# Attention with both heads of a pair in one step: 64-column value matmuls on the two halves of a PSUM bank, and softmax divisors summed by GpSimd and VectorE

## The chip, the cores and the metric

One core of a Trainium2 chip runs the whole program. The metric is the device time of one execution in microseconds, median of the runs.

## The reference

Two layers of a decoder trunk over 1024 tokens, width 1024, 16 heads of 64 dimensions, all in float32. Layer 0 has three attention branches that gates add up: compressed keys ("cmp"), full causal attention (every one of the 16 selected blocks is there, so the selection is the whole causal range) and a sliding window of 512 ("near"). Layer 1 is masked attention with one key and value of 64 dimensions shared by all heads, where a mask leaves each query its 256 best keys. After each attention comes an output projection and a gated ConvFFN. What the change touches is this part, of either layer:

```
s = jnp.where(mask, einsum(q, k), NEG_INF)
p = softmax(s)
o = einsum(p, v)
```

The kernel computes exp(s - peak) without dividing, sums it over the keys, and divides the product with v by that sum at the end.

## The kernel before, in words

**Tiling.** Attention goes over 16 rounds (`ROUNDS`): a round is one pair of heads and one half (512 queries) of the tokens. In a round, a branch ("rb" counts round and branch) is worked off in units. A unit is one head and one block of 128 keys against the queries that see it: 512, 384, 256 or 128 of them (`key_blocks`). In the first half a branch has 4 blocks of 512, 384, 256 and 128 queries; in the second, "full" has 8 (five of 512) and "near" 8 (two each of 512, 384, 256 and 128). A "cmp" branch is a single unit for both heads.

**A unit.** TensorE: `scores_pe` writes the scores, transposed (keys on partitions), to one of three PSUM banks by two float32r matmuls (L866 of high and L868 of low parts) and bf16 matmuls that add the mask (L872). ScalarE: `exp_act` (L910) writes the exponentials to one of four buffers PX. TensorE: `values_pe` (L890) multiplies them, in float32, by a stationary operand V of 128 columns: 64 of values and 64 of ones. So partitions 0 to 63 of the result are the product and partition 64 is the sum of the probabilities: the divisor costs no matmul of its own. The result accumulates in bank 6 or 7, by head in turn. "cmp" has its product (L884) in bank 6 and its divisors, by a matmul with ones (L885), in bank 7.

**Around it.** The order is written out by unit: at step s TensorE does the scores of unit s+2, then what the planner (`AttentionPlan`, with a cost in microseconds for each unit) has put in ring slot s, then the values of unit s. The ring is three more PSUM banks, in which TensorE computes the untransposed scores of a coming round (`peak_pe`, L813) and VectorE takes their row maxima (`peak_dve`, L1002); a transpose (L832) and a DMA put the maxima into the low query operand. When a branch closes, `evict_act` copies divisor and product per head (L933, L934, for cmp L929, L930), the SyncE queue sends the divisors through DRAM (L1092, L1097, L1103), VectorE takes the reciprocal (`sums_dve`) and applies it (`apply_dve`, L1037, L1041), and ScalarE and VectorE split the result into high and low parts HH and HL (L942, L1047) for the output projection. In layer 1 VectorE and ScalarE also finish four mask tiles during attention, at the steps of `LATE_MASKS`; VectorE's part is L2234 to L2242.

**The output projection** (`outproj_pe`) takes 16 weight tiles k. Tiles 0 and 1 are loaded before attention, 2 and 3 after it (`attention_sp`, end); GpSimd splits the first three into high and low parts (`split`, L455 and L458), ScalarE and VectorE the others (L467, L474). Before tile 4 the SyncE queue waits for the last HL and restores the 4 MB residual XT (L1109).

The value matmul, with its ones column inside V, is:

```
V = B[a.keys[n.kind][2]]
last = nc.tensor.matmul(PS[:, 6 + n.g % 2, n.c0:n.c0 + n.w], V[:, g, n.kb, :], probs,
                        start=n.first, stop=n.last)
```

## Time and profile before

| | |
|---|---|
| median of 3 runs | 3381.35 us (3377.76 to 3383.71) |
| profiled execution | 3380.0 us, its span 3378.2 us |
| attention of layer 0 in the span | 327 to 884 us |
| attention of layer 1 in the span | 2185 to 2493 us |
| TensorE busy (matmul) | 2992.9 us, 89% |
| VectorE busy | 2085.6 us, 62% |
| ScalarE busy | 1512.3 us, 45% |
| GpSimd busy | 279.4 us, 8% |
| mean granted TensorE clock | 0.937 of full speed |

PE is TensorE's matmul, PEld its weight load, DVE VectorE, ACT ScalarE, POOL GpSimd, SPq the SyncE queue that issues DMAs. A float32 matmul leaves two records of weight load and two of matmul in the trace, a float32r or bf16 matmul one of each. A record of a matmul lasts longer than the time in which it holds up the next one; the start of the next weight load or matmul tells that time.

### The profile page before, as it was taken

Reading aid. Unit: us, or ns where it says so; the run is one execution under the profiler, and the core shown is the slowest. Engines: PE = TensorE matmul, PEld = TensorE weight load, DVE = VectorE, ACT = ScalarE, POOL = GpSimd, SP = SyncE. Lnnn points to the kernel's source line nnn. Section 1 sums busy time; section 2 is a strip of 40 time slices with the busy share of each in tenths; the row PEclk is TensorE's granted clock in tenths of the full one; section 3 lists DMA queues with packets and bytes.
Section 4 is the critical chain, followed back from the end, with each engine's and each line's share of the span. In section 5 each row is a group of like instructions: output and inputs, shape, how many; then the busy total and the mean of one; then the engine's idle time right before and its main releaser. Section 6 shows DMA issues by size and latency. Waiting matters only on the chain.

```text
span 3378.2 us, 37432 instructions
## 1 busy us (share of the span) xinstructions
PE 2992.9 (89%) x13312; PEld 2299.4 (68%) x13312; DVE 2085.6 (62%) x3708; ACT 1512.3 (45%) x2609; POOL 279.4 (8%) x221
## 2 busy tenths in 40 slices
PE   7797999999879999999968664389997999999997
PEld 5685666666667888878856553256666788887885
DVE  6544445555266766677675699664326676667656
ACT  4342554455444544444433544344434454444443
POOL 2352000000000000000003035300000000000000
PEclk9787999999989999999989787689998999999999
DMA  5143211121322333333323012332132233333332
GB/s 165 44 105 97 50 47 39 42 52 36 110 75 88 95 93 100 95 92 96 98 69 96 0 54 84 94 70 54 39 104 75 88 94 94 100 95 93 99 109 73
DMA packets 360178, 270.45 MB, mean 80 GB/s; under 512 B 63942, under 2 KB 313864, under 8 KB 359480
## 3 DMA queue, kind: packets, MB, share of 16 engines
q1 hardware_dynamic: 358839, 265.96, 27.4%
q8 instruction: 106, 1.74, 0.2%
q10 hardware_dynamic: 1152, 2.10, 0.2%
q14 instruction: 81, 0.66, 0.1%
HBM read 233.46 MB, written 29.82 MB: 78 GB/s over the span
## 4 chain that ended last, share of the span: by engine, by line
PE 77%; DVE 9%; ACT 4%; issue 3%; DMA 3%; POOL 3%; SPq 1%; POOLq 0%; ACTq 0%; DVEq 0%
PE PS L485 18%; PE PS L487 18%; PE PS L486 18%; PE PS L890 10%; PE PS L813 3%; PE PS L868 3%; PE PS L866 3%; PE PS L872 2%; SPq L1912 1%; DVE m_Z L2285 1%; DVE RT_b L590 1%; DMA WL<-ql_save 1%; POOL m_QS L1929 1%; PE PS L639 1%; PE PS L884 0%
## 5 line engine op out<-in xcount | busy, mean ns | idle before, releaser
L485 PE MATMUL PS<-HH,WH 128*128 128x512 f32 (+1 forms) x2160 | 859.1, 398 | 133.9 <-POOL WL L458 90.3
L486 PE MATMUL PS<-HL,WH 128*128 128x512 f32 (+1 forms) x2160 | 850.7, 394 | 0.0
L487 PE MATMUL PS<-HH,WL 128*128 128x512 f32 (+1 forms) x2160 | 849.6, 393 | 0.0
L485 PEld LDWEIGHTS PS<-HH,WH 128*128 128x128 f32 x2160 | 415.9, 193 | 228.2 <-issue 96.9
L486 PEld LDWEIGHTS PS<-HL,WH 128*128 128x128 f32 x2160 | 415.5, 192 | 87.1 <-issue 2.5
L487 PEld LDWEIGHTS PS<-HH,WL 128*128 128x128 f32 x2160 | 414.4, 192 | 86.6
L474 DVE TENSOR_TENSOR WL<-WR,WH 128x1024 fp32r<-128x1024 f32 x290 | 354.2, 1221 | 109.4 <-ACT WH L467 97.8
L467 ACT ACTIVATE WH<-WR 128x1024 fp32r<-128x1024 f32 x290 | 308.1, 1062 | 124.4 <-PE PS L487 89.9
L910 ACT ACTIVATE n_PX<-PS 128x512 f32<-128x512 f32 (+3 forms) x400 | 186.7, 468 | 256.7 <-PE PS L872 205.3
L1002 DVE CUSTOM_DVE_ANT_0 n_JUNK<-PS,n_MZ 128x512 bf16<-128x512 f32 (+2 forms) x320 | 148.6, 488 | 134.1 <-PE PS L813 132.6
L454 POOL TENSOR_TENSOR TOUCH<-WR 128x1 f32<-128x1 f32 x45 | 12.0, 267 | 2030.4 <-PE PS L487 1031.3
L890 PE MATMUL PS<-m_PX,m_V 128*128 128x512 f32 (+3 forms) x384 | 165.5, 514 | 9.7 <-ACT m_PX L910 9.7
L890 PE MATMUL PS<-n_PX,n_VS 128*128 128x512 f32 (+3 forms) x384 | 162.5, 505 | 10.7 <-ACT n_DR L930 10.7
L1342 DVE TENSOR_TENSOR Y_c<-PS,Y_c 128x512 f32<-128x512 f32 x160 | 107.0, 688 | 88.0 <-PE PS L487 87.6
L1342 DVE TENSOR_TENSOR Y_b<-PS,Y_b 128x512 f32<-128x512 f32 x160 | 107.0, 688 | 87.3 <-PE PS L487 86.9
L910 ACT ACTIVATE m_PX<-PS 128x512 f32<-128x512 f32 x192 | 93.1, 488 | 137.5 <-PE PS L872 137.0
L1002 DVE CUSTOM_DVE_ANT_0 m_JUNK<-PS,m_MASK 128x512 bf16<-128x512 f32 (+3 forms) x160 | 89.9, 595 | 100.0 <-PE PS L813 99.9
L485 PE MATMUL PS<-HIDH_b,WH 128*128 128x512 f32 x352 | 142.4, 405 | 6.3 <-issue 3.2
L485 PE MATMUL PS<-HIDH_c,WH 128*128 128x512 f32 x352 | 141.9, 403 | 3.9 <-issue 3.2
L890 PE MATMUL PS<-n_PX,n_VW 128*128 128x128 f32 (+3 forms) x384 | 140.4, 448 | 0.0
L487 PE MATMUL PS<-HIDH_b,WL 128*128 128x512 f32 x352 | 139.8, 397 | 0.0
L486 PE MATMUL PS<-HIDL_b,WH 128*128 128x512 f32 x352 | 139.7, 397 | 0.0
(375 smaller groups left out, 5373.3 us busy)
## 6 DMA issues: line engine op xcount, KB each, us to landing
WR<-in_ffn_w_up SPq DMA_DIRECT2D x176, 512.0 KB, 3.8
WR<-in_ffn_w_down SPq DMA_DIRECT2D x88, 512.0 KB, 3.6
WH<-qh_save SPq DMA_DIRECT2D x64, 256.0 KB
n_RB<-r_save SPq DMA_DIRECT2D x96, 128.0 KB, 3.0
WR<-in_nsa_w_out SPq DMA_DIRECT2D x16, 512.0 KB, 4.1
WL<-ql_save SPq DMA_DIRECT2D x32, 256.0 KB
WR<-in_dsa_w_in SPq DMA_DIRECT2D x16, 512.0 KB, 4.4
WR<-in_dsa_w_out SPq DMA_DIRECT2D x16, 512.0 KB, 4.2
```

Source lines behind the costliest of these rows:

```text
L467: nc.scalar.activation(WH[:, x, :], WR[:, r, :], ACT.Copy).then_inc(w_hi, 1)
L474: nc.vector.tensor_tensor(WL[:, x, :], WR[:, r, :], WH[:, x, :].bitcast(F32), ALU.subtract).then_inc(w_split, 1)
L485: nc.tensor.matmul(dst, wh, xh, start=start, stop=False)
L486: nc.tensor.matmul(dst, wh, xl, start=False, stop=False)
L487: return nc.tensor.matmul(dst, wl, xh, start=False, stop=stop)
L813: last = nc.tensor.matmul(PS[:, 3 + y % 3, 0:w], query_high(p.r, p.h, p.ii * P, P), KA[:, g, k0:k0 + w], start=True, stop=True)
L866: nc.tensor.matmul(dst, KA[:, g, keys], query_high(n.r, n.h, n.c0, n.w), start=True, stop=False)
L868: last = nc.tensor.matmul(dst, KB[:, g, keys], query_low(n.r, n.h, n.c0, n.w), start=False, stop=not masks)
L890: last = nc.tensor.matmul(PS[:, 6 + n.g % 2, n.c0:n.c0 + n.w], V[:, g, n.kb, :], probs, start=n.first, stop=n.last)
L910: nc.scalar.activation(a.B["PX"][:, u % 4, 0:n.w], PS[:, u % 3, 0:n.w], ACT.Exp).then_inc(a_ex, 1)
L1002: nc.vector.tensor_tensor_reduce(out=B["JUNK"][:, x % 2, 0:w], in0=src, in1=mask, scale=1.0, scalar=-3e38, op0=ALU.add, op1=ALU.max, accum ...
L1342: nc.vector.tensor_tensor(y, bank(4 + x % 3), y, ALU.add).then_inc(f.da, 1)
```

## The change

A step now takes one key block of both heads (an item; in cmp, as before, the one unit).

- **Scores**: two sets per item, each in one of the same three banks, one item ahead (it was two units).
- **Values**: V has 64 columns, no ones. Two float32 matmuls per item, head 0 to partitions 0 to 63 and head 1 to partitions 64 to 127 of one bank, for 288 items. The branches take banks 6 and 7 in turn, cmp too.
- **Divisors**: the exponentials of a branch's first block go to a buffer ACC, one per head; those of later blocks to PX (now six buffers), and are added to ACC by GpSimd (head 0, `add_pool`) and VectorE (head 1, `add_dve`): 240 additions on each. Two steps after a branch has closed, `divisors_pe` multiplies ACC by ones, 64 columns per head side by side in a bank of the scores: 48 pairs of matmuls. cmp has its one matmul with ones there.
- **Evictions**: one of the product and one of the divisors per branch instead of two each for two heads.
- **Waits**: the exponentials wait for the additions and values of three items before; TensorE waits for both exponentials of an item, and for the additions before a divisor. The projection waits for the last divisor's eviction.
- **Weights**: output tiles 2 and 3 are loaded during attention, and tiles 0 to 2 are split by ScalarE and VectorE there instead of by GpSimd.
- **Planner**: a table of costs per item instead of per unit, `LATE_MASKS` at other steps.

```diff
+PARTS = 6
+Item = namedtuple("Item", "r kind kb c0 w diag far first last rb u px")
...
+        self.divisor_step = {rb: s + 2 for rb, s in self.closes.items()}
...
-            cost = 3.4 if u.kind == "cmp" else max(0.7, 1.6 * u.w / HALF + dense * u.w / P)
+            cost = 2.1 if x.kind == "cmp" else max(1.1, 2.2 * x.w / HALF + 2 * dense * x.w / P)
+            self.begin.append(self.begin[-1] + cost + 0.9 * len(self.divisors_at.get(s, ())))
...
-        for rb, x in self.closes.items():
-            t = self.begin[x + 1]
+        for rb, s in self.divisor_step.items():
+            t = self.begin[min(s + 1, self.NI)] + 1.5 * max(s + 1 - self.NI, 0)
...
+        self.weights_at = {self.ends[13] + 2: 0, self.ends[14] + 2: 1, self.ends[15] + 1: 2}
...
-                ("VS", [P, 2, QT, P], F32), ("VW", [P, 2, QT, P], F32), ("VC", [P, 2, P], F32),
+                ("VS", [P, 2, QT, DH], F32), ("VW", [P, 2, QT, DH], F32), ("VC", [P, 2, P], F32),
...
-                    ("PX", [P, 4, HALF], F32), ("OP", [P, ns, HALF], F32), ("DR", [P, ns, HALF], F32),
+                    ("PX", [P, PARTS, HALF], F32), ("ACC", [P, na, HALF], F32), ("OP", [P, ns, HALF], F32), ("DR", [P, ns, HALF], F32),
...
+            for h in range(2):
+                u = n.u + h
+                bank_free(pe, a, u)
+                dst = PS[:, u % 3, 0:n.w]
+                nc.tensor.matmul(dst, KA[:, g, keys], query_high(n.r, h, n.c0, n.w),
                                  start=True, stop=False)
...
+        def values_pe(pe, a, s):
+            n = a.plan.items[s]
+            B, g = a.B, a.group(a.order[n.r][0])
+            b = 6 + n.rb % 2
+            if n.first and n.rb >= 2:
+                pe.wait_ge(a_ov, a.rb0 + n.rb - 1)
+            if n.kind == "cmp":
+                pe.wait_ge(a_ex, a.qk0 + n.u + 1)
+                nc.tensor.matmul(bank(b), B["VC"][:, g, :], a.probabilities(n, 0), start=True,
+                                 stop=True).then_inc(a_pv, 1)
+                return
+            pe.wait_ge(a_ex, a.qk0 + n.u + 2)
+            V = B[a.keys[n.kind][2]]
+            for h in range(2):
+                last = nc.tensor.matmul(PS[64 * h:64 * h + 64, b, n.c0:n.c0 + n.w], V[:, g, n.kb, :],
+                                        a.probabilities(n, h), start=n.first, stop=n.last)
+            last.then_inc(a_pv, 1)
+
+        def divisors_pe(pe, a, rb):
+
+            u = a.plan.divisor_unit[rb]
+            bank_free(pe, a, u)
+            if a.plan.kinds[rb % a.nb] == "cmp":
+                nc.tensor.matmul(bank(u % 3), a.B["ONB"][:, :], a.total(rb, 0), start=True,
+                                 stop=True).then_inc(qk, 1)
+                return
+            for h in range(2):
+                pe.wait_ge(a_added[h], a.added0 + a.plan.added[rb] // 2)
+                last = nc.tensor.matmul(PS[64 * h:64 * h + 64, u % 3, :], ONES[:, 0:DH], a.total(rb, h),
+                                        start=True, stop=True)
             last.then_inc(qk, 1)
...
-        def values_pe(pe, a, u):
-            n = a.plan.units[u]
-            B, g = a.B, a.group(a.order[n.r][0])
-            pe.wait_ge(a_ex, a.qk0 + u + 1)
-            probs = B["PX"][:, u % 4, 0:n.w]
-            if n.kind == "cmp":
-                if n.g:
-                    pe.wait_ge(a_ov, a.ov0 + n.g)
-                nc.tensor.matmul(bank(6), B["VC"][:, g, :], probs, start=True, stop=True)
-                last = nc.tensor.matmul(bank(7), B["ONB"][:, :], probs, start=True, stop=True)
-            else:
-                if n.first and n.g >= 2:
-                    pe.wait_ge(a_ov, a.ov0 + n.g - 1)
-                V = B[a.keys[n.kind][2]]
-                last = nc.tensor.matmul(PS[:, 6 + n.g % 2, n.c0:n.c0 + n.w], V[:, g, n.kb, :], probs,
-                                        start=n.first, stop=n.last)
-            last.then_inc(a_pv, 1)
 
...
+            scores_pe(pe, a, 0)
+            for s in range(plan.NI + 2):
+                if s + 1 < plan.NI:
+                    scores_pe(pe, a, s + 1)
                 ring_pe(pe, a, s)
-                values_pe(pe, a, s)
-
-        def exp_act(act, a, u):
-            n = a.plan.units[u]
-            act.wait_ge(qk, a.qk0 + u + 1)
-            if u >= 4:
-                act.wait_ge(a_pv, a.qk0 + u - 3)
-            nc.scalar.activation(a.B["PX"][:, u % 4, 0:n.w], PS[:, u % 3, 0:n.w],
-                                 ACT.Exp).then_inc(a_ex, 1)
+                if s < plan.NI:
+                    values_pe(pe, a, s)
+                for rb in plan.divisors_at.get(s, ()):
+                    divisors_pe(pe, a, rb)
+
+        def exp_act(act, a, s):
+            n = a.plan.items[s]
+            for h in range(1 if n.kind == "cmp" else 2):
+                if not n.first and n.px + h >= PARTS:
+                    act.wait_ge(a_pv, a.pv0 + a.plan.part_item[n.px + h - PARTS] + 1)
+                    act.wait_ge(a_added[h], a.added0 + (n.px - PARTS) // 2 + 1)
+                act.wait_ge(qk, a.qk0 + n.u + h + 1)
+                nc.scalar.activation(a.probabilities(n, h), PS[:, (n.u + h) % 3, 0:n.w],
+                                     ACT.Exp).then_inc(a_ex, 1)
+
+        def added_total(engine, a, s, h):
+
+            n = a.plan.items[s]
+            if a.plan.items[s - 1].first:
+                engine.wait_ge(a_pv, a.pv0 + s)
+            engine.wait_ge(a_ex, a.qk0 + n.u + h + 1)
+            if n.px:
+                engine.wait_ge(a_added[h], a.added0 + n.px // 2)
+            return a.total(n.rb, h)[:, n.c0:n.c0 + n.w]
+
+        def add_pool(pool, a, s):
+            n = a.plan.items[s]
+            if not n.first:
+                total = added_total(pool, a, s, 0)
+                nc.gpsimd.tensor_tensor(total, total, a.probabilities(n, 0), ALU.add).then_inc(a_added[0], 1)
+
+        def add_dve(dve, a, s):
+            n = a.plan.items[s]
+            if not n.first:
+                total = added_total(dve, a, s, 1)
+                nc.vector.tensor_tensor(total, total, a.probabilities(n, 1), ALU.add).then_inc(a_added[1], 1)
...
-        def evict_act(act, a, u):
-            n = a.plan.units[u]
-            slot = n.rb % a.ns
-            act.wait_ge(a_pv, a.qk0 + u + 1)
-            if n.h == 0 and n.rb >= a.ns:
-                act.wait_ge(a_tm, a.rb0 + n.rb - a.ns + 1)
-            OP, DR = a.B["OP"], a.B["DR"]
-            if n.kind == "cmp":
-                nc.scalar.activation(OP[:, slot, :], bank(6), ACT.Copy)
-                nc.scalar.activation(DR[:, slot, :], bank(7), ACT.Copy).then_inc(a_ov, 2)
-            else:
-                b, o = 6 + n.g % 2, 64 * n.h
-                nc.scalar.activation(DR[o:o + 1, slot, :], PS[64:65, b, :], ACT.Copy)
-                nc.scalar.activation(OP[o:o + 64, slot, :], PS[0:64, b, :], ACT.Copy).then_inc(a_ov, 1)
+        def evict_act(act, a, rb):
+
+            slot = rb % a.ns
+            act.wait_ge(a_pv, a.pv0 + a.plan.closes[rb] + 1)
+            if rb >= a.ns:
+                act.wait_ge(a_tm, a.rb0 + rb - a.ns + 1)
+            nc.scalar.activation(a.B["OP"][:, slot, :], bank(6 + rb % 2), ACT.Copy).then_inc(a_ov, 1)
+
+        def divisors_act(act, a, rb):
+
+            u = a.plan.divisor_unit[rb]
+            act.wait_ge(qk, a.qk0 + u + 1)
+            nc.scalar.activation(a.B["DR"][:, rb % a.ns, :], bank(u % 3), ACT.Copy).then_inc(a_ex, 1)
...
+                if s in plan.weights_at:
+                    high_split_act(act, a.infos["out"][plan.weights_at[s]])
...
+                if 0 <= s < plan.NI:
+                    add_dve(dve, a, s)
                 if a.n == 1 and s in LATE_MASKS:
                     mask_dve(dve, LATE_MASKS[s])
+                if s in plan.weights_at:
+                    low_split_dve(dve, a.infos["out"][plan.weights_at[s]])
...
+            for s in range(a.plan.NI):
+                add_pool(pool, a, s)
...
+                for rb in plan.divisors_at.get(s, ()):
                     slot = rb % a.ns
-                    sp.wait_ge(a_ov, a.ov0 + 2 * (rb + 1))
+                    sp.wait_ge(a_ex, a.qk0 + plan.divisor_unit[rb] + 1)
...
+                if plan.weights_at.get(s - 2) in (0, 1):
+                    k = 2 + plan.weights_at[s - 2]
+                    load(sp, a.infos["out"][k], wout(k), DT)
...
-            for k in range(2, 4):
-                load(sp, a.infos["out"][k], wout(k), DT)
...
+                if k == 0:
+                    pe.wait_ge(a_ex, a.qk0 + a.plan.units)
...
-        LATE_MASKS = {3: 4, 14: 5, 25: 6, 36: 7}
+        LATE_MASKS = {2: 4, 7: 5, 13: 6, 19: 7}
...
-            for x in L0["out"][0:3]:
-                split(pool, x)
```

TensorE in layer 1, second half of the tokens, between two rounds. Before, each row of `m_V` is one head's value matmul of one unit:

```order
L890 MATMUL PS<-m_PX,m_V 128x512
L866 MATMUL PS<-WH,m_KDA 128x512
L868 MATMUL PS<-WL,m_KDB 128x512
L872 MATMUL PS<-m_IDB,m_MASK 128x128 x4
L813 MATMUL PS<-m_KDA,WH 128x384
L813 MATMUL PS<-m_KDA,WH 128x512
L890 MATMUL PS<-m_PX,m_V 128x512
```

Now (L913, L915, L919 are the scores, L851 the peaks, L937 the values, L951 the divisors):

```order
L937 MATMUL PS<-m_PX,m_V 64x512 x2
L951 MATMUL PS<-m_ACC,ONES 64x512 x2
L913 MATMUL PS<-WH,m_KDA 128x512
L915 MATMUL PS<-WL,m_KDB 128x512
L919 MATMUL PS<-m_IDB,m_MASK 128x128 x4
L913 MATMUL PS<-WH,m_KDA 128x512
L915 MATMUL PS<-WL,m_KDB 128x512
L919 MATMUL PS<-m_IDB,m_MASK 128x128 x4
L851 MATMUL PS<-m_KDA,WH 128x512
L851 MATMUL PS<-m_KDA,WH 128x256
L851 MATMUL PS<-m_KDA,WH 128x512
L937 MATMUL PS<-m_PX,m_V 64x512 x2
```

Between two groups of full-width matmuls (128 columns of weights) now stands one group of matmuls with 64 columns, where one matmul with 128 stood between every set of scores.

VectorE in layer 1, at the first of the four late mask tiles. Before (ISA rows are the peaks):

```order
L1002 ISA m_JUNK,m_NM<-PS,m_MASK 128x512
L1002 ISA m_NM 128x1
L2234 TENSOR_SCALAR m_E1<-m_Z,m_THV 128x640
L2235 TENSOR_SCALAR m_R,m_CNT<-m_Z,m_THV 128x640
L2237 TENSOR_SCALAR m_NEED<-m_CNT 128x1
L2239 SCALAR_TENSOR_TENSOR m_R<-m_E1 128x640
L2240 SCALAR_TENSOR_TENSOR m_E1<-m_R,m_NEED,m_E1 128x640
L2242 SCALAR_TENSOR_TENSOR m_MASK<-m_Z,m_THV,m_E1 128x640
L1002 ISA m_JUNK,m_NM<-PS,m_MZ 128x128
```

Now (L999 are the additions, L2330 to L2338 the mask, L1092 the peaks):

```order
L999 TENSOR_TENSOR m_ACC<-m_ACC,m_PX 128x256
L2330 TENSOR_SCALAR m_E1<-m_Z,m_THV 128x640
L2331 TENSOR_SCALAR m_R,m_CNT<-m_Z,m_THV 128x640
L2333 TENSOR_SCALAR m_NEED<-m_CNT 128x1
L2335 SCALAR_TENSOR_TENSOR m_R<-m_E1 128x640
L2336 SCALAR_TENSOR_TENSOR m_E1<-m_R,m_NEED,m_E1 128x640
L2338 SCALAR_TENSOR_TENSOR m_MASK<-m_Z,m_THV,m_E1 128x640
L1092 ISA m_JUNK,m_NM<-PS,m_MASK 128x384
L1092 ISA m_NM 128x1
L999 TENSOR_TENSOR m_ACC<-m_ACC,m_PX 128x128
```

The mask work of a tile now stands between two additions, and exponentials are queued behind those additions by the new wait.

## Rows read from the trace of the kernel before

**Rows 1.** The page: busy time of each engine, and the chain that ended last.
```profile
PE 2992.9 (89%) x13312; PEld 2299.4 (68%) x13312; DVE 2085.6 (62%) x3708; ACT 1512.3 (45%) x2609; POOL 279.4 (8%) x221
PE 77%; DVE 9%; ACT 4%; issue 3%; DMA 3%; POOL 3%; SPq 1%; POOLq 0%; ACTq 0%; DVEq 0%
```

**Rows 2.** Windows: layer 0's attention, layer 1's start and rest, layer 0's first projection.
```profile
core 0: us, PE busy (x) PEld busy (x) DVE busy (x) ACT busy (x) POOL busy (x), PEclk, DMA share, GB/s
327.00:884.00 557.00, 527.88 (x2518) 351.49 (x2517) 273.90 (x891) 283.69 (x585) 7.11 (x6) 1.00 0.18 42
2180.00:2280.00 100.00, 83.51 (x422) 58.49 (x421) 61.21 (x179) 45.21 (x98) 0.00 (x0) 0.85 0.28 62
2280.00:2493.00 213.00, 205.04 (x1107) 129.07 (x1106) 80.60 (x271) 96.88 (x190) 7.15 (x6) 1.00 0.17 40
884.00:925.00 41.00, 32.99 (x132) 26.02 (x133) 10.91 (x16) 11.04 (x17) 3.54 (x3) 0.92 0.61 192
```

**Rows 3.** PE groups by shape: line, out<-in, shape, xcount | busy us, mean ns | idle before.
```profile
L890 PE MATMUL PS<-m_PX,m_V 128*128 128x512 f32 x192 | 103.1, 619 | 4.6 <-ACT m_PX L910 4.6
L890 PE MATMUL PS<-n_PX,n_VS 128*128 128x512 f32 x192 | 102.7, 617 | 10.7 <-ACT n_DR L930 10.7
L890 PE MATMUL PS<-n_PX,n_VW 128*128 128x512 f32 x96 | 51.7, 620 | 0.0
L890 PE MATMUL PS<-n_PX,n_VW 128*128 128x384 f32 x96 | 39.5, 492 | 0.0
...
L890 PE MATMUL PS<-m_PX,m_V 128*128 128x384 f32 x64 | 27.7, 516 | 0.0
...
L884 PE MATMUL PS<-n_PX,n_VC 128*128 128x512 f32 x32 | 17.5, 627 | 11.8 <-ACT n_OP L934 11.8
```

**Rows 4.** Timeline of PE and its weight loads at the end of layer 0's attention.
```profile
884.93 1.02 PE L885 MATMUL PS<-n_PX,n_ONB 128*128 128x512 f32 x2
884.93 0.19 PEld L885 LDWEIGHTS PS<-n_PX,n_ONB 128*128 128x128 f32 x1 [0.24 <-issue]
885.36 0.19 PEld L485 LDWEIGHTS PS<-HH,WH 128*128 128x128 f32 x1 [0.24 <-issue]
...
886.25 0.40 PE L487 MATMUL PS<-HH,WL 128*128 128x512 f32 x1
...
886.48 0.40 PE L485 MATMUL PS<-HH,WH 128*128 128x512 f32 x1
```

**Rows 5.** Timeline of POOL and DVE in layer 0's attention, two instructions that overlap.
```profile
843.93 2.34 POOL L458 TENSOR_TENSOR WL<-WR,WH 128x1024 fp32r<-128x1024 f32 x1
844.67 2.15 DVE L1037 TENSOR_TENSOR n_T<-n_OP,n_RB 128x512 f32<-128x512 f32 x1 [2.52 <-DMA n_RB<-r_save]
```

**Rows 6.** Durations at 128x512: a DVE product alone, POOL and ACT groups.
```profile
877.37 0.69 DVE L1037 TENSOR_TENSOR n_T<-n_OP,n_RB 128x512 f32<-128x512 f32 x1 [5.71 <-DMA n_RB<-r_save]
...
L1552 POOL TENSOR_TENSOR n_ROTQ<-n_ROTQ,n_SIN 128x512 f32<-128x512 f32 x16 | 21.1, 1320 | 46.5 <-ACT n_ROTQ L734 46.4
...
L910 ACT ACTIVATE m_PX<-PS 128x512 f32<-128x512 f32 x96 | 57.1, 595 | 73.2 <-PE PS L872 73.0
```

**Rows 7.** Timeline of PE and DVE at a late mask tile of layer 1.
```profile
2227.85 1.15 DVE L2240 SCALAR_TENSOR_TENSOR m_E<-m_R,m_NEED,m_E 128x896 f32<-128x896 f32 x1
2229.03 1.15 DVE L2242 SCALAR_TENSOR_TENSOR m_MASK<-m_Z,m_THV,m_E 128x896 bf16<-128x896 f32 x1
...
2231.71 2.07 PE L890 MATMUL PS<-m_PX,m_V 128*128 128x512 f32 x2 [4.64 <-ACT m_PX L910]
```

**Rows 8.** Timeline after layer 0's attention: TensorE's wait, the restore's issue, tile 4's split.
```profile
904.88 0.80 PE L485 MATMUL PS<-HH,WH 128*128 128x512 f32 x1 [8.01 <-POOL WL L458]
...
901.23 0.34 SPq L1109 DMA_DIRECT2D XT_b<-x_save  x1
...
915.30 1.06 ACT L467 ACTIVATE WH<-WR 128x1024 fp32r<-128x1024 f32 x1 [10.60 <-DMA WR<-in_nsa_w_out]
```

More of the change, by code:

```diff
@@ L109, in key_blocks, with attention_items @@
     return blocks
-def attention_units(kinds, order):
-    units, groups = [], 0
+def attention_items(kinds, order):
+    items = []
     for r in range(ROUNDS):
@@ L157, in __init__ @@
-        self.ends = {r: max(x for x, u in enumerate(self.units) if u.r == r) for r in range(ROUNDS)}
-        self.closes = {u.rb: x for x, u in enumerate(self.units) if u.last}
+        self.items, self.peaks = attention_items(kinds, order), attention_peaks(kinds, order)
+        self.NI = len(self.items)
+        self.closes = {x.rb: s for s, x in enumerate(self.items) if x.last}
+        self.divisor_step = {rb: s + 2 for rb, s in self.closes.items()}
+        self.divisors_at = {}
+        for rb, s in self.divisor_step.items():
+            self.divisors_at.setdefault(s, []).append(rb)
@@ new lines, in __init__ @@
+        self.number()
+        self.begin = [0.0]
+        for s, x in enumerate(self.items):
+            cost = 2.1 if x.kind == "cmp" else max(1.1, 2.2 * x.w / HALF + 2 * dense * x.w / P)
+            self.begin.append(self.begin[-1] + cost + 0.9 * len(self.divisors_at.get(s, ())))
+        self.opens = {r: min(s for s, x in enumerate(self.items) if x.r == r) for r in range(ROUNDS)}
+        self.ends = {r: max(s for s, x in enumerate(self.items) if x.r == r) for r in range(ROUNDS)}
+        self.last_unit = {r: max(x.u + (x.kind != "cmp") for x in self.items if x.r == r) for r in range(ROUNDS)}
@@ L159, in __init__, with number @@
         self.place_peaks()
         self.place_chains()
+    def number(self):
+        unit, parts = 0, 0
+        self.divisor_unit = {}
+        for s in range(-1, self.NI + 2):
+            if s + 1 < self.NI:
+                x = self.items[s + 1]
+                paired = x.kind != "cmp"
+                self.items[s + 1] = x._replace(u=unit, px=None if x.first else parts)
+                unit += 1 + paired
+                parts += 0 if x.first else 2
+            for rb in self.divisors_at.get(s, ()):
+                self.divisor_unit[rb] = unit
+                unit += 1
+        self.units, self.parts = unit, parts
+        self.added, total = {}, 0
+        for x in self.items:
+            total += 0 if x.first else 2
+            self.added[x.rb] = total
+        self.part_item = [s for s, x in enumerate(self.items) if not x.first for _ in range(2)]
@@ L683, in trunk @@
                                           "mc", "me", "ex", "pv", "ov"))
+        a_added = [semaphore(f"a_added{h}") for h in range(2)]
         a_rc, a_rr, a_tm, a_tt, a_hh, a_hl = (
@@ L702, in __init__ @@
                 self.ready0 = 5 * n
-                self.qk0 = sum(x.NU for x in before)
+                self.qk0 = sum(x.units for x in before)
+                self.pv0 = sum(x.NI for x in before)
+                self.added0 = sum(x.parts // 2 for x in before)
                 self.pk0 = sum(len(x.ring) for x in before)
@@ L782, in load_queries_sp @@
             else:
[L783 removed]
+                sp.wait_ge(qk, a.qk0 + a.plan.last_unit[r - 3] + 1)
             high = qh_save[k].rearrange("(h d) t -> d h t", h=2)
@@ L2498, in _ @@
             attention_pool(pool, A0)
-            for x in L0["out"][0:3]:
-                split(pool, x)
             prep1["pool"](pool)
             attention_pool(pool, A1)
-            for x in L1["out"][0:3]:
-                split(pool, x)
         @block.scalar
```

122 lines of the change are left out of this document (57 added, 65 removed).

## Prediction

> **What bounds the kernel now.** I read the page first: TensorE is busy 89% of the span and holds 77% of the chain that ended last [rows 1]. Then the windows by stage, because a share over the whole span says nothing about attention: in layer 0's attention TensorE is busy 528 of 557 us, at full granted clock, in layer 1's second part 205 of 213, with VectorE at 49% and 38% and ScalarE at 51% and 45% [rows 2]. So there TensorE's own work sets the time. Layer 1's first 100 us are different: TensorE is busy 83.5 of them and VectorE 61, with the late masks among it. Then the groups by shape, to count the value matmuls, and the timeline, to price one [rows 3, 4].
>
> **What a value matmul costs.** The weight load of the second record of a float32 matmul starts at 884.93 and that of the next instruction at 885.36 [rows 4]: each of the two records (a pass) holds TensorE for 0.43 us at 512 columns. The mean of 620 ns in the group counts flight time that overlaps the next matmul. Narrower passes take proportionally less (a rough rule here; some weight loads show through at 128). Count in full-width passes: 480 records at 512 columns (192 + 192 + 96), and 224 each at 384, 256 and 128 (96 for `n_VW`, 64 each for `n_VS` and `m_V`; the groups not shown have the counts of the shown one) [rows 3]. That is 480 + 224 x 1.5 = 816 passes, or 351 us, for one head at a time.
>
> **The change, part by part.**
>
> *Values and divisors.* Per item the same four passes remain (two heads, two records each), on half the columns of the array. The 48 new divisor pairs add 192 passes at full width; cmp's matmul with ones is only moved. So 1008 passes are issued, and all hangs on how many run at a time. No row shows a matmul with 64 columns. Bounds from the nearest row: nothing overlaps, 0.43 us for each pass (1.72 us for a full-width item and its two heads); or the two heads overlap entirely, 0.86 us. I take the second: the two matmuls use different columns of weights, different partitions of the bank and different operands, so nothing in the program makes one wait for the other. 504 passes instead of 816: -312 x 0.43 = **-134 us**. The other end is +192 x 0.43 = +83 us.
>
> *Eviction waits.* cmp used banks 6 and 7 both and so waited for the head evicted before it: 11.8 us before L884 and 10.7 us before the next branch's first value matmul [rows 3]. Now the branches alternate banks, and a bank's eviction is a whole branch old when it is needed: **-22 us**. Nothing is late behind it, since the scores and the exponentials of those steps were done.
>
> *Fewer evictions.* ScalarE drops two of four copies for each of 48 branches. It isn't the bound at half load: 0. Exponentials take 0.6 us at full width [rows 6], 1.2 for an item, which lies beside two sets of scores, the peaks and the values, over 2 us.
>
> *Additions on GpSimd.* 240 of them; in layer 0, 160, which are 100 of full width by columns. At 1.32 us [rows 6] that is some 135 to 150 us of 440: it keeps up, and the divisor matmul two steps after the close doesn't wait for it: 0.
>
> *Additions on VectorE.* At 0.69 us [rows 6] the 160 of layer 0 take 70 to 80 us. But two engines now read pairs of SBUF operands at once, and one row shows what that does: a product that takes 0.69 us alone took 2.15 when it began during GpSimd's two-input subtraction, and ended 0.55 us after it (846.82 against 846.27) [rows 5]. Head 1's exponential ends 0.6 us after head 0's, so its addition will find GpSimd 0.6 us into 1.3 and end 0.55 us after it: about 1.25 us instead of 0.69 at full width, less at the narrow ones. Over layer 0 that is about 50 us more. VectorE then has 274 + 78 + 50 = 400 us [rows 2] in what would be 557 - 22 - 86 = 450 us (86 being layer 0's share of the passes, 528 - 264 - 64 = 200 fewer). At 90% its jitter reaches TensorE, through the peaks and the new wait of the exponentials. I put **+15 us**; bounds 0 and 40.
>
> *The late masks.* In layer 1 a mask tile holds VectorE for 5 to 7 us (two of its instructions take 1.15 us each), and TensorE waited 4.64 us at one [rows 7]. Additions and, three items on, exponentials now queue behind it too. These waits stay, some grow, and what TensorE saves in the first 100 us is partly waited away: **+10 us**; bounds 0 and 25.
>
> *Hand-over.* TensorE waits once per item for both exponentials instead of once per head, one item ahead instead of two units, the same depth. 0.03 us is an estimate for a weight load not hidden, and the divisors' eviction holds a bank of the scores: for 336 groups **+5 us**; bounds 0 and 0.1 x 336 = 34.
>
> *The projection's weights.* TensorE waits 8.0 us for tile 2's split after attention [rows 8], and the change removes that. But tile 4's data comes behind the 4 MB restore, which waits for the last HL (issued 901.23), and lands at 915.3 [rows 8]. The end of that chain, eviction, divisors, reciprocal, product, isn't shorter. TensorE will run tiles 2 and 3 earlier and wait before tile 4 instead: **0**, bounds -13 (both layers) and +4. The splits moved to ScalarE and VectorE (three per layer of 1.06 and 1.2 us) and the two loads earlier on the SyncE queue lie beside attention: 0.
>
> Sum: -134 - 22 + 15 + 10 + 5 = -126 us. Against the profiled execution's 3380.0 us that is **3254 us**. The median of the runs shown, 3381.35, is 0.04% from it, so I make no correction. A measurement of this kernel can tell about 0.2% (7 us) from no change. The case's own range, from the bounds above, is 3225 to 3310.
>
> **The rivals.**
>
> *Three slots out of four.* The order on TensorE is head 0's two passes, then head 1's two. Every pass in the trace starts after the one before it in program order. If a pass that must wait for its own half of the array also holds the passes behind it, only head 0's second pass and head 1's first overlap: 756 passes. -60 x 0.43 = -26, -22 for the evictions, nothing for a crowded VectorE, +5 for the masks: 3337 us, and up to 3371 with 0.1 us per group for weight loads. The Trainium skill says under "TensorE: Matmul & The Clock Gate", part 3, that matmuls on different tiles of the array overlap but start and end strictly in program order; by it this rival, not full overlap, would be the forecast. No run here shows it yet.
>
> *Nothing overlaps.* This is the rival on the other side, and also the case that the change doesn't do what it says. The place is each item's value pair, the price 0.43 us for each of 192 added passes: +83 - 22 + 10 + 5 gives 3456 us. For it: no row shows two matmuls streaming at once. It decides from the point where a full-width pair takes more than 3.2 to 3.3 passes, 1.4 us.
>
> *A change of shape empties the array.* A matmul's record lasts 0.40 us while the next starts 0.23 us later [rows 4], so 0.17 us of one lies under the next. 288 items mean 576 changes between full-width and 64-column matmuls. If each must drain what is in flight, that costs 576 x 0.17 = 98 us; if the weight load of 0.19 us can't be ahead either, 207 us. With full overlap and VectorE no longer crowded, 3254 - 15 + 98 = 3337 to 3446 us; it turns the change into a loss from 0.22 us per change. "TensorEngine Tiling (Array Packing)" in the Trainium skill says under Key Properties that changing the tiling mode drains TensorE; that is the rule that speaks against this change, and no row of this kernel shows a change of mode.
>
> **How the numbers follow.** Full overlap 0.38, three slots 0.15, nothing overlaps 0.22, drained changes 0.25. Faster by over 0.2%: nearly all of the first, two thirds of the second, a third of the fourth, 0.55. Within 0.2%: 0.07, from the edges of the second and fourth. Slower: 0.38, the third, half of the fourth, and mishaps of the rest. Both signs hold much of the chance, so the likeliest case's range of 3225 to 3310 stands beside the one that holds 8 in 10: 3225 to 3460, which takes in all four cases and leaves out drained changes with no or little overlap and the worst of the masks.
>
> **What would show it.** Right: for a full-width item of layer 1 the next scores' weight load starts 0.9 us after the values' first one, with matmul records of both heads overlapping in time; the window of layer 0's attention shrinks from 557 to about 460 us with VectorE near 90% busy, additions on VectorE at 1.2 us; waits for n_OP and n_DR before value matmuls are gone; the 8 us before tile 2 reappears before tile 4. Three slots: 1.3 us for that item. None: 1.7 us. Drained: a gap of 0.2 us or more before each group of 64 columns and behind it, whatever the pairs do. The forecast is wrong if the items take over 1.1 us, or if the wait before values goes to exponentials that wait for an addition.

## The result, and the profile after

The changed kernel takes 3412.36 us, median of 4 runs (3406.58 to 3414.04); the kernel before took 3382.53 us beside it. The ratio is 1.0088, 95% interval 1.0075 to 1.0100: slower by 0.9%, about 30 us, where 126 us of gain were forecast. The profiled execution took 3414.04 us, its span 3412.2 us. The page of after, busy time and chain:

```profile
PE 2999.0 (88%) x13504; PEld 2191.8 (64%) x13504; DVE 2232.3 (65%) x3951; ACT 1453.2 (43%) x2519; POOL 490.9 (14%) x443
...
PE 71%; DVE 10%; DMA 6%; issue 4%; ACT 4%; POOL 3%; SPq 2%; DVEq 0%; ACTq 0%; POOLq 0%
```

Against [rows 1] TensorE lost six points of the chain, and DMA transfers gained three. The windows of after, columns as in [rows 2], layer 0's attention, layer 1's start and rest, the first projection:

```profile
331.00:908.00 577.00, 526.49 (x2630) 277.30 (x2626) 362.28 (x1036) 239.20 (x520) 151.35 (x160) 0.95 0.19 42
2182.00:2290.00 108.00, 71.94 (x345) 38.98 (x345) 55.00 (x163) 29.28 (x66) 18.54 (x20) 0.75 0.32 77
2290.00:2523.00 233.00, 218.09 (x1256) 111.10 (x1254) 146.69 (x385) 97.12 (x197) 70.33 (x65) 0.96 0.20 51
908.00:945.00 37.00, 28.75 (x116) 21.50 (x113) 9.73 (x15) 11.00 (x18) 0.00 (x0) 0.92 0.53 178
```

Layer 0's attention takes 20 us longer than the 557 of [rows 2] and not 100 less. VectorE is busy 63%, not near 90%. And the granted clock, 1.00 before, is 0.95: that has no term in my sum. From the start of the first matmul with `n_MZ` (the mask of "full" and "near") to that of the last, layer 0 takes 592.7 us against 565.8; from the first peak matmul to the last mask matmul, layer 1 takes 323.4 against 320.3. So +27 and +3 us, and the loss is all there.

**The two heads do run at once.** The timeline of after, TensorE, an item of layer 1 with the divisors behind it (start, us). The value records are shown as three windows merge them, the first, the first two, and the first three; the others follow in order:

```profile
2442.84 0.64 PE L937 MATMUL PS<-m_PX,m_V 128*64 128x512 f32 x1
...
2442.84 0.65 PE L937 MATMUL PS<-m_PX,m_V 128*64 128x512 f32 x2
...
2442.84 1.07 PE L937 MATMUL PS<-m_PX,m_V 128*64 128x512 f32 x3
...
2443.74 1.03 PE L951 MATMUL PS<-m_ACC,ONES 128*64 128x512 f32 x4
...
2444.70 0.19 PEld L913 LDWEIGHTS PS<-WH,m_KDA 128*128 128x128 f32 x1 [0.81 <-issue]
2444.70 0.51 PE L913 MATMUL PS<-WH,m_KDA 128*128 128x512 f32 x1
...
2445.05 0.40 PE L915 MATMUL PS<-WL,m_KDB 128*128 128x512 f32 x1
```

Two records together end 0.65 us after 2442.84, as one alone does, so the second starts at the same time; the third ends 0.43 us later. Four value passes hold TensorE from 2442.84 to 2443.74, 0.9 us, and four divisor passes 0.86. That is the 504 slots of the forecast. The Trainium skill, "TensorE: Matmul & The Clock Gate", part 3, says that such matmuls start and end strictly in program order; I had read that pass by pass, which would have given three slots for four passes, and the trace has two. Matmul by matmul the trace doesn't contradict it.

**And each group of 64 columns has a gap behind it.** The last divisor pass starts at 2444.17 (0.43 before the end of its slot at 2444.60). The scores' weight load, which before came a whole pass early [rows 4], starts at 2444.70; and the second score matmul, which should follow the first by 0.23 us, follows by 0.34. In all 0.22 us.

To add this up I took the start of every TensorE record in attention, and what lies between it and the end of the streaming time of the records before. Streaming is 0.43 us a pass at 512 columns as in [rows 4], half of that for a float32r or bf16 matmul, and less in proportion with fewer columns. Where the granted clock was at its lower level, 1.2 GHz, a pass of 512 columns holds TensorE twice as long: here the second pair of value passes starts at 435.38 and the first of the divisors 0.86 us later.

```profile
435.38 1.06 PE L937 MATMUL PS<-n_ACC,n_VS 128*64 128x512 f32 x2
436.24 1.70 PE L951 MATMUL PS<-n_ACC,ONES 128*64 128x512 f32 x4
```

What this adds to streaming is the column "lower clock". The sums by size of gap, in us:

| | streaming | lower clock | gaps under 0.3 us | 0.3 to 0.8 | over 0.8 | all |
|---|---|---|---|---|---|---|
| layer 0 before | 454 | 6 | 68 | 18 | 20 | 566 |
| layer 0 after | 368 | 34 | 131 | 8 | 52 | 593 |
| layer 1 before | 245 | 12 | 30 | 3 | 30 | 320 |
| layer 1 after | 197 | 20 | 62 | 12 | 32 | 323 |

So streaming fell by 86 and 48 us, 134 as forecast. Small gaps gave back 95, larger ones 33, and the lower clock 36. In layer 0 the small gap behind the values has a median of 0.22 us where it had 0.02, and the one ahead of them 0.10 to 0.18, by what stands before, where it had 0.00 to 0.09.

**The long waits are new ones.** The timeline of after at one of them, in layer 0 (start, us, and in brackets the idle time before and who ended it), with windows of 4 us behind it:

```profile
430.80 0.69 DVE L1127 TENSOR_TENSOR n_TMP<-n_OP,n_RB 128x512 f32<-128x512 f32 x1 [3.75 <-DMA n_RB<-r_save]
...
431.59 0.60 ACT L1015 ACTIVATE n_OP<-PS 128x512 f32<-128x512 f32 x1 [4.84 <-DVE n_TMP L1127]
432.08 1.08 ACT L976 ACTIVATE n_ACC<-PS 128x512 f32<-128x512 f32 x2
...
432.73 0.50 PE L913 MATMUL PS<-WH,n_KSA 128*128 128x512 f32 x1 [3.11 <-ACT n_ACC L976]
```
```profile
428.00:432.00 4.00, 1.62 (x6) 0.68 (x4) 1.16 (x2) 0.41 (x1) 0.00 (x0) 1.00 0.83 207
432.00:436.00 4.00, 3.25 (x10) 1.64 (x12) 3.87 (x18) 1.17 (x3) 0.00 (x0) 0.77 0.40 87
436.00:440.00 4.00, 4.00 (x15) 1.60 (x13) 1.82 (x4) 3.59 (x7) 1.62 (x2) 0.80 0.01 0
```

Read upwards: a broadcast of divisors lands late, so VectorE's product is late, so ScalarE's eviction waits 4.84 us for an output slot, two exponentials stand behind it, and TensorE's scores wait 3.11 us for a bank. Then the granted clock is 0.77 and 0.80 over 8 us: part of the time at 1.2 GHz, a further 1.7 us lost. Divisors used to be evicted with their block; now they come two steps later and the chain behind them starts later.

**Layer 1's two halves part.** Windows over its first eight rounds, with the late masks, and its last eight, before first, then after:

```profile
2171.00:2293.00 122.00, 101.17 (x510) 70.17 (x510) 69.07 (x208) 55.10 (x118) 0.00 (x0) 0.84 0.32 71
2293.00:2492.00 199.00, 191.40 (x1024) 119.34 (x1024) 76.31 (x257) 88.47 (x173) 7.15 (x6) 1.00 0.15 36
```
```profile
2198.00:2344.00 146.00, 115.87 (x556) 61.38 (x556) 80.49 (x241) 43.63 (x100) 18.47 (x24) 0.80 0.27 64
2344.00:2523.00 179.00, 174.16 (x1041) 88.71 (x1042) 118.39 (x303) 81.21 (x161) 63.02 (x56) 1.00 0.17 43
```

The last eight rounds, at full clock in both, won 20 us: the change paid there. The first eight lost 24.

The projection behaves as forecast (after, timeline): the 8.01 us before tile 2 [rows 8] are gone and 6.68 us stand before tile 4, at the end of 4 MB of restore.

```profile
912.87 0.47 PE L510 MATMUL PS<-HH,WH 128*128 128x512 f32 x1 [1.16 <-ACT n_DR L1021]
...
941.57 0.80 PE L510 MATMUL PS<-HH,WH 128*128 128x512 f32 x1 [6.68 <-DVE WL L499]
```

### The profile page after: what moved, and what is told of

Same layout as the page of the kernel before. It is cut to its first block, busy times and chain, and to the rows that moved or that the text cites. A ratio compares the mean times of both kernels' runs of the same rounds, so it can differ in the third digit from the quotient of the medians.

```text
span 3412.2 us, 38564 instructions
## 1 busy us (share of the span) xinstructions
PE 2999.0 (88%) x13504; PEld 2191.8 (64%) x13504; DVE 2232.3 (65%) x3951; ACT 1453.2 (43%) x2519; POOL 490.9 (14%) x443
## 4 chain that ended last, share of the span: by engine, by line
PE 71%; DVE 10%; DMA 6%; issue 4%; ACT 4%; POOL 3%; SPq 2%; DVEq 0%; ACTq 0%; POOLq 0%
PE PS L510 18%; PE PS L511 18%; PE PS L512 18%; PE PS L937 5%; PE PS L913 3%; PE PS L851 3%; PE PS L915 2%; DMA n_RB<-r_save 1%; PE PS L919 1%; PE PS L951 1%; SPq L2008 1%; DMA WL<-ql_save 1%; DMA r_save<-n_R 1%; DVE RT_b L615 1%; DVE m_Z L2381 1%
## 5 line engine op out<-in xcount | busy, mean ns | idle before, releaser
L499 DVE TENSOR_TENSOR WL<-WR,WH 128x1024 fp32r<-128x1024 f32 x296 | 361.6, 1222 | 127.1 <-ACT WH L492 122.1
L993 POOL TENSOR_TENSOR n_ACC<-n_ACC,n_PX 128x384 f32<-128x384 f32 (+3 forms) x160 | 151.3, 946 | 468.3 <-ACT n_PX L976 261.8
L1092 DVE CUSTOM_DVE_ANT_0 n_JUNK<-PS,n_MZ 128x512 bf16<-128x512 f32 (+2 forms) x320 | 146.2, 487 | 98.3 <-PE PS L851 97.8
L976 ACT ACTIVATE n_PX<-PS 128x384 f32<-128x384 f32 (+3 forms) x320 | 134.1, 438 | 135.8 <-PE PS L919 132.4
L512 PE MATMUL PS<-HIDH_c,WL 128*128 128x512 f32 x352 | 139.4, 396 | 0.0
L511 PE MATMUL PS<-HIDL_c,WH 128*128 128x512 f32 x352 | 139.3, 396 | 0.0
L993 POOL TENSOR_TENSOR m_ACC<-m_ACC,m_PX 128x512 f32<-128x512 f32 (+3 forms) x80 | 81.5, 1019 | 251.6 <-ACT m_PX L976 156.3
L1092 DVE CUSTOM_DVE_ANT_0 m_JUNK<-PS,m_MASK 128x512 bf16<-128x512 f32 (+3 forms) x160 | 87.7, 594 | 41.9 <-PE PS L851 41.6
```

The costliest lines, as they stand in the source:

```text
L499: nc.vector.tensor_tensor(WL[:, x, :], WR[:, r, :], WH[:, x, :].bitcast(F32), ALU.subtract).then_inc(w_split, 1)
L511: nc.tensor.matmul(dst, wh, xl, start=False, stop=False)
L512: return nc.tensor.matmul(dst, wl, xh, start=False, stop=stop)
L976: nc.scalar.activation(a.probabilities(n, h), PS[:, (n.u + h) % 3, 0:n.w], ACT.Exp).then_inc(a_ex, 1)
L993: nc.gpsimd.tensor_tensor(total, total, a.probabilities(n, 0), ALU.add).then_inc(a_added[0], 1)
L1092: nc.vector.tensor_tensor_reduce(out=B["JUNK"][:, x % 2, 0:w], in0=src, in1=mask, scale=1.0, scalar=-3e38, op0=ALU.add, op1=ALU.max, accum ...
```

## The experiments

Theory D: changes between full-width and 64-column matmuls cost the time. Its rivals, S (longer steps and later exponentials), E (the output slots) and A, V or P (the additions), are named in each expectation. All results are medians of 4 to 10 runs. "Before" beside them was 3378.78 to 3380.22 us, and 3382.53 beside after; a difference to after's 3412 below compares medians of different times and is uncertain by these 2 to 4 us.

**1. Only the shape, in the kernel before.** Edit, with the two evictions reading the same rows:

```diff
-last = nc.tensor.matmul(PS[:, 6 + n.g % 2, n.c0:n.c0 + n.w], V[:, g, n.kb, :], probs,
+last = nc.tensor.matmul(PS[64 * n.h:64 * n.h + 64, 6 + n.g % 2, n.c0:n.c0 + n.w], V[:, g, n.kb, 0:DH], probs,
```

> The kernel before with one edit: each value matmul uses the first 64 columns of V alone and writes 64 PSUM rows, head 0 the lower, head 1 the upper ones. The divisors are left out (the row that was a divisor is now a row of the values). Nothing overlaps, the 816 + 816 passes, the units and all waits stay. Theory D (a change between full-width and 64-column matmuls costs TensorE time by itself, about 0.09 us more on the way in and 0.20 us more on the way out, as read from the trace of after): 576 groups x 0.29 = +167 us, so 3480 to 3570, with the gap from the last pass to the next score matmul near 0.2 us. Theory S (the gaps of after come from its longer steps and its later exponentials, not from the shape): 3370 to 3390, gaps as before. An end between, 3400 to 3450, would say that a part of the cost was hidden by waits.

Measured: 3544.82 us, ratio 1.0482 (1.0464 to 1.0499), +165 us. For 576 groups that is 0.286 us each, and not clock: the granted clock of layer 0's attention is 0.99 for 0.98 before. Theory S falls as the cause of the small gaps. The price explains the last eight rounds of layer 1: 88 passes fewer are 38 us, 64 groups cost 18, and 20 were won. The same step in both timelines, before first, then the experiment (values at 384 columns, scores at 512):

```profile
553.51 0.81 PE L890 MATMUL PS<-n_PX,n_VW 128*128 128x384 f32 x2
553.87 0.69 PE L866 MATMUL PS<-WH,n_KWA 128*128 128x512 f32 x1
554.40 0.39 PE L868 MATMUL PS<-WL,n_KWB 128*128 128x512 f32 x1
```
```profile
559.72 0.86 PE L890 MATMUL PS<-n_PX,n_VW 128*64 128x384 f32 x2
560.51 0.50 PE L866 MATMUL PS<-WH,n_KWA 128*128 128x512 f32 x1
560.84 0.40 PE L868 MATMUL PS<-WL,n_KWB 128*128 128x512 f32 x1
```

From the first pass to the second score matmul 0.89 us became 1.12, with the same columns streamed.

**2. Half as many changes of shape.** Values of two key blocks behind one another:

```diff
+            self.values_at.setdefault(s if x.last or index % 2 else s + 1, []).append(s)
...
-                if s < plan.NI:
-                    values_pe(pe, a, s)
+                for t in plan.values_at.get(s, ()):
+                    values_pe(pe, a, t)
```

> After, with the values of two key blocks behind one another (scores s+1, scores s+2, values s-1, values s), so half as many changes of shape and the same passes. Theory D: 144 groups fewer x 0.29 to 0.37 = -42 to -53 us against after, 3355 to 3375, and so below the kernel before; less if the two score groups in a row wait for a free bank. Theory S: no gain, or a loss of 10 to 30 us since exponentials have less cover (3410 to 3445).

Measured: 3392.16 us, ratio 1.0035 (1.0023 to 1.0046), so -20 against after's 3412. Small gaps fell as theory D has it, 131 to 105 us in layer 0 and 62 to 48 in layer 1: 40 us, where the trace has 157 runs of 64-column matmuls for 284 (some divisors now stand alone). But only layer 0 got shorter (565 us for 593). In layer 1 gaps over 0.8 us grew from 32 us to 45: there the two sets of scores have no values between them, and the longest wait of scores for an exponential is 6.4 us for 5.0. Waits of layer 1, after first, then the experiment (waiter, line, waited for: us, times, longest):

```profile
PE PS L913 <- ACT m_PX L976: 9.9, 5, 5.0
```
```profile
PE PS L917 <- ACT m_PX L980: 19.2, 6, 6.4
```

**3. One more slot for the evicted sums.** DR and RB keep their slots, so their wait moves to the divisor copy:

```diff
-            if rb >= a.ns:
-                act.wait_ge(a_tm, a.rb0 + rb - a.ns + 1)
+            if rb >= a.ns + 1:
+                act.wait_ge(a_tm, a.rb0 + rb - a.ns)
...
```

> After with one more slot for the evicted sums; the wait for the product of an earlier block moves from the eviction to the divisor copy two steps later. The trace of after has ScalarE waiting 45.8 us at this place. Theory E (these waits hold up exponentials and so scores): -15 to -35 us, 3377 to 3397, and the waits on L1127 gone. Theory D alone: the waits have other cover, or come back at the divisor copy: -0 to -8 us, 3404 to 3412.

Measured: 3389.90 us, ratio 1.0031 (1.0019 to 1.0043), -22: theory E holds, beside D. Waits of ScalarE for an output slot in layer 0, after first:

```profile
ACT n_OP L1015 <- DVE n_TMP L1127: 45.8, 13, 4.8
```
```profile
ACT n_OP L1015 <- DVE n_TMP L1129: 14.3, 7, 3.0
```

Layer 0 takes 569 us for 593. Its gaps over 0.8 us fell from 52 to 37, and the mean granted clock of its attention rose from 0.93 (313 to 906) to 0.96, by the table's reckoning 12 us less at the lower clock: about half of the gain is clock that came back with the waits gone.

**4. No additions.** The waits on them in TensorE and ScalarE go too:

```diff
-                if 0 <= s < plan.NI:
-                    add_dve(dve, a, s)
...
-            for s in range(a.plan.NI):
-                add_pool(pool, a, s)
```

> After without the additions on GpSimd and VectorE and the waits on them. The divisors are then those of the first key block alone, plus 1.0 in the copy. Theory A (additions crowd VectorE and hold up peaks or probability buffers): -30 us or more, 3380 or less, and the waits of scores for exponentials and of the transpose for peaks go. Theory D+E (changes of shape and late output slots): at most -5 to -20, 3392 to 3408, with the small gaps (under 0.3 us) of the key block loop unchanged.

Measured: 3369.30 us, ratio 0.9976 (0.9964 to 0.9988), -43. Twice what I gave them: theory A is right in size. The small gaps stayed, 129 us for 131 in layer 0, so this is no part of D; those over 0.3 us fell from 59 to 43, and the time lost to the lower clock from 34 to 13. But ScalarE's waits for a slot stayed too (44.4 us), which theory A doesn't explain by itself.

**5. Which engine's additions?** Three kernels: GpSimd's left out; all on GpSimd; all on VectorE. The last two compute everything.

```diff
-            for s in range(a.plan.NI):
-                add_pool(pool, a, s)
...
-                total = added_total(dve, a, s, 1)
-                nc.vector.tensor_tensor(total, total, a.probabilities(n, 1), ALU.add).then_inc(a_added[1], 1)
+                for h in range(2):
+                    total = added_total(dve, a, s, h)
+                    nc.vector.tensor_tensor(total, total, a.probabilities(n, h), ALU.add).then_inc(a_added[h], 1)
```

> After without GpSimd's additions (head 0's divisors are those of the first key block alone, plus 1.0 in the copy); VectorE's stay. The additions cost 43 us together. Theory V (the price is VectorE's time, in whose queue peaks stand behind an addition): 3395 to 3412, next to nothing won. Theory P (GpSimd slows VectorE, or holds probability buffers): 3370 to 3385, with VectorE's 512-column addition down from 0.84 to 0.98 us to about 0.69.

> After with the additions of both heads on GpSimd; the computation is whole. Theory V: 3375 to 3390, since VectorE is as free as without additions, unless GpSimd's 2.5 to 2.8 us for a 512-column item makes it the bound in layer 1 (then exponentials wait for probability buffers and divisors for sums, and it gives back 10 to 30). Theory P: slower than after, 3415 to 3440.

> After with the additions of both heads on VectorE; the computation is whole. Theory V: the price of one more head's additions, +25 to +45 us, 3437 to 3457. Theory P: with GpSimd idle each addition takes 0.69 us and not 0.84 to 0.98, so the sum of both is hardly over the one: 3395 to 3420.

Measured: 3373.33 us (3367.10 to 3386.58), 3385.73 (3377.82 to 3390.13) and 3385.24 (3378.27 to 3389.38). Without GpSimd's share, and the waits for it, 39 of the 43 us are gone, while VectorE still adds for its head; these runs scatter by 19 us, and the profiled one is the slowest. Either engine alone does all of the additions for 27 us less than the two together. Theory V falls: twice the additions on VectorE are cheaper. GpSimd's own length isn't it either, since twice its additions are cheaper too. It is the pair that costs. VectorE in layer 0, after, then all on VectorE:

```profile
L1092 DVE CUSTOM_DVE_ANT_0 n_JUNK<-PS,n_MZ 128x512 bf16<-128x512 f32 x108 | 73.8, 689 | 35.3 <-PE PS L851 35.2
L999 DVE TENSOR_TENSOR n_ACC<-n_ACC,n_PX 128x512 f32<-128x512 f32 x40 | 36.3, 906 | 0.1
L1131 DVE TENSOR_TENSOR n_T<-n_T,n_TMP 128x512 f32<-128x512 f32 x30 | 27.4, 915 | 1.0
```
```profile
L1000 DVE TENSOR_TENSOR n_ACC<-n_ACC,n_PX 128x512 f32<-128x512 f32 x80 | 51.4, 685 | 0.0
L1133 DVE TENSOR_TENSOR n_T<-n_T,n_TMP 128x512 f32<-128x512 f32 x32 | 22.1, 692 | 1.1
```

With GpSimd adding, a VectorE addition of two SBUF tiles takes 906 ns, and the sum in the divisor chain 915 instead of 692; the peak, with PSUM as its main input, takes 689 beside GpSimd as well. The Trainium skill, "SBUF — State Buffer", says under "SBUF: two separate sides" that VectorE with two SBUF inputs and a GpSimd instruction that reads SBUF take turns for whole instructions; by it the first to start makes the other wait, and the trace agrees. Theory P had VectorE alone: half right, because all on GpSimd, which still meets VectorE's chain (924 ns for the same sum), gained as much. In layer 0 the gain is in part clock in both: 34 us lost to the lower clock in after, 15 with all on GpSimd and 22 with all on VectorE. How the longer VectorE instructions reach TensorE no run takes apart.

**6. The plan.** Items and divisors dearer in the plan, so that its reckoning of time fits:

```diff
-            cost = 2.1 if x.kind == "cmp" else max(1.1, 2.2 * x.w / HALF + 2 * dense * x.w / P)
-            self.begin.append(self.begin[-1] + cost + 0.9 * len(self.divisors_at.get(s, ())))
+            cost = 3.0 if x.kind == "cmp" else max(1.6, 3.2 * x.w / HALF + 2 * dense * x.w / P)
+            self.begin.append(self.begin[-1] + cost + 1.3 * len(self.divisors_at.get(s, ())))
```

> After with the planner's costs raised (a 512-column item 2.2 to 3.2, compressed 2.1 to 3.0, divisors 0.9 to 1.3), since its plan adds up to 387 us where layer 0 takes 593, and the kernel before's to 501 where it took 566. Peaks then start about a third fewer steps ahead, and the divisor chain ends a third fewer steps behind its block. Theory E (products too late hold output slots): as the extra slot, -15 to -30 us, 3380 to 3398. Rival: peaks get too late, and the transposes and the first scores of a round wait: +0 to +20.

Measured: 3424.07 us, ratio 1.0138 (1.0123 to 1.0153), +12: a miss for my theory, a hit for its rival. ScalarE's waits for a slot in layer 0 fell as with the slot, to 17.9 us, but they moved: VectorE now waits for the broadcast, and peaks stand behind it. Waits in layer 0 of this kernel (in after the first was 24.2 and the second 23.3):

```profile
DVE n_TMP L1127 <- DMA n_RB<-r_save: 73.9, 30, 4.6
PEld PS L851 <- DVE n_NM L1092: 42.3, 49, 3.4
```

Layer 0 still got 6 us shorter (586 us for 593). The loss lies in layer 1's last eight rounds: from the eighth eviction to the last 204 us for 179, while the eight before, from the first exponential on, took 128 for 137. There TensorE's peak matmuls wait for VectorE to free a bank, after first, then the experiment:

```profile
PE PS L851 <- DVE m_NM L1092: 3.8, 15, 0.8
```
```profile
PE PS L851 <- DVE m_NM L1092: 22.1, 29, 8.6
```

**7. Combinations** of the edits above, and in the third also peaks placed earlier:

```diff
-            due = self.begin[max(self.opens[self.peaks[x].r] - 1, 0)] - 7.0
+            due = self.begin[max(self.opens[self.peaks[x].r] - 1, 0)] - 9.0
```

> After with both the pairs of value groups and the extra output slot. If the two causes are apart, their gains add (-20 and -22 as measured): 3365 to 3375, below the kernel before. If both took from the same waits: 3380 to 3392.

> As before this one, with the planner's costs raised too. Theory E: the plan does what the slot does, so no more than -10 against it: 3355 to 3372. Rival (late peaks): slower than it by 5 to 20.

> Both changes that helped (pairs of value groups, one more output slot; 3367 as measured) and peaks placed 9.0 instead of 7.0 of the plan's microseconds ahead of their round. Costlier, hence later, peaks cost 43 us on top of the same two, so if peaks are still late, earlier ones give 5 to 15: 3352 to 3362. If they are not: 3363 to 3372, or more where query slots or the three banks of the ring hold them up.

> Pairs of value groups, one more output slot, and the additions of both heads on VectorE, none on GpSimd; the computation is whole. If the three causes are apart, the gains of -20, -22 and -27 against after add up to -69: 3335 to 3350, about 1.1 per cent under the kernel before. If the chain of products and the crowded VectorE are the same waits (the extra slot already gives slack to what VectorE does late): 3350 to 3367. VectorE's additions of 512 columns at 0.69 us, as with GpSimd idle.

Measured: 3367.14, 3410.40, 3408.65 and 3362.48 us. Pairs of values and the slot add up (-45, where -20 and -22 are -42), and the kernel is faster than before, ratio 0.9958 (0.9944 to 0.9972). The plan's costs take 43 of them back. Earlier peaks take 41 back, where I expected 5 to 15 of gain: in layer 0 transposes wait 20 us for VectorE instead of 11, and the granted clock in its attention is 0.92 instead of 0.96; half of the loss is in layer 1 (344 us for 323, from the first peak to the last mask). Why peaks placed either way cost some 40 us I leave open. The last one, with all additions on VectorE, has the lowest median of the kernels that compute everything, ratio 0.9952 (0.9939 to 0.9966), but it isn't clear of the first: its third cause brought 5 us and not 27, and the runs of the two overlap (3361.58 to 3367.27, and 3359.97 to 3369.68). That the slack from the output slot already covered what VectorE did late would explain it, and isn't shown.

## Why the prediction was wrong

**The step that failed is the hand-over**, with the rival I held apart from it: I forecast "the same depth", +5 us for 336 groups, bounds 0 and 34. A group of 64 columns between full-width matmuls costs 0.29 us by itself (experiment 1), 82 us for the 288 items; the trace of after has 95 more of small gaps. That is the rival "a change of shape empties the array". Its price per change of 0.17 to 0.35 was too high, 0.14 to 0.15 was measured, and I gave it 0.25 and full overlap without it 0.38. That its range of 3337 to 3446 holds the result is luck: with the measured price its own sum is 3254 - 15 + 82 = 3321 us, and the other 91 us came from waits, additions and the clock. Of its sign, 0.2 us or more before and behind each group, the gap behind came (0.22) and the one ahead fell a little short. It should have been the likeliest of the rivals: the row that priced it, a record of 0.40 us under a pitch of 0.23 [rows 4], was in hand, nothing in the trace spoke against it, and "TensorEngine Tiling (Array Packing)" in the Trainium skill, Key Properties, says it drains. I took the lack of a row as evidence for no cost.

- *Values and divisors*: right, -134.
- *Eviction waits*: the 22 us before L884 and L890 are gone, but a new wait came on the same engine. I asked who waits for a bank and not who waits for OP's slot, whose release moved two steps further back. 22 us, in no term.
- *Additions on GpSimd*, costed at 0 since it keeps up: that cover was the wrong question. It does keep up, and taking its share out won 39 us. That VectorE has to take turns with it is seen in the lengths (906 ns for 685); how much of the 39 us that makes isn't shown.
- *Additions on VectorE*: +15, bounds 0 and 40; both engines' together measured 43. The mechanism of [rows 5] was right, its reach too large: a mean of 906 ns and not 1.25 us, VectorE at 63% and not 90%.
- *The clock*: no term. In layer 0's attention it is 0.93 for 0.98 before; the lower clock costs 28 us more there and 8 more in layer 1. That is more than the larger gaps themselves (33). Part of it is inside the prices of the slot and the additions, which fell with it.
- *Late masks*: +10, bounds 0 and 25. The first eight rounds of layer 1 save 24 passes (10 us) and pay 32 groups (9 us), and lost 24 us: some 25 us for masks, waits and the clock there, which no experiment takes apart. Without additions they still took 20 us longer than before, from the first exponential to the eighth eviction (133 for 113).
- *Projection weights*: right, 0, with the wait where it was forecast.

The recorded arithmetic has three slips, none of which would have saved the forecast. The 0.03 us of the hand-over came from no row, and 336 times it is 10 us, not 5. All bounds taken together give 3211 to 3327 us, not 3225 to 3310. And drained changes with VectorE no longer crowded turn into a loss from 0.24 us per change, not 0.22.

The sum with measured prices, and the masks' 25 us as the remainder that they are: -134 - 22 + 82 + 43 + 22 + 25 = +16 us, where +30 came. The 14 us between are open; small gaps are 13 us above the 82. The single prices are no exact terms of a sum, as the last combination shows, and the clock and the masks have no experiment of their own. The table adds up fully, but names no causes beyond the shape: streaming -134, small gaps +95, larger ones +33, lower clock +36.

## What to carry over

Packing two narrow matmuls side by side pays for the passes, but each narrow group between full-width work has a fixed price (0.29 us here): compare the passes saved per group with it, and put groups together before counting on the gain. Where SBUF pairs are added beside the tensor work, try one of VectorE and GpSimd, whichever, and not both: here that was 27 us, but no gain clear of the scatter once values were paired and the slot added. When a result is taken later than before, follow every slot it holds to the engine that waits for it, and to what stands in that engine's queue. And count the clock beside a wait: about half of what the extra slot won was clock.

## What the runs showed of the hardware

- Two float32 matmuls on the two column halves of the array overlap pass by pass: four passes in two slots of 0.43 us, although each matmul's two passes stand behind one another in the program.
- Leaving 64-column work costs 0.22 us where leaving full-width values cost 0.02, and entering it about 0.09 more than entering those; over 576 groups the whole kernel lost 0.286 us each.
- A wait of 3.1 us of TensorE was followed by a granted clock of 0.77 to 0.80 over 8 us in the profile: 1.7 us lost, over half of the wait again. At 1.2 GHz a float32 pass of 512 columns held TensorE for 0.86 us instead of 0.43.
- A VectorE addition of two SBUF tiles of 128x512 takes 685 ns with GpSimd idle and 906 in the mean beside GpSimd's additions; a peak with PSUM as its main input takes 689 in both.
